# A feed-forward stage in wide units: the first weight sum made by an accumulating DMA instead of a VectorE addition

## The chip, the cores and the metric

One Trainium2 chip, one of its cores. The metric is the device time of one execution in microseconds (us); the median of several runs counts.

## The reference, cut to what matters

One layer of a hybrid backbone over 640 tokens (512 latent, 128 context) with 1024 channels: modulation from a conditioning vector, three mixing branches (neighbourhood attention, mLSTM, short convolution) merged by gates, an output projection, and then the feed-forward stage that the change is in:

```
h2 = rmsnorm(x, P['g_pre_ffn'][l]) * (1 + scale2) + shift2
ff = (jax.nn.silu(h2 @ P['w_ffn_gate'][l]) * (h2 @ P['w_ffn_up'][l])) @ P['w_ffn_down'][l]
x = x + gate2 * rmsnorm(ff, P['g_post_ffn'][l])
```

The gate and up matrices are 1024 x 2816, in float32.

## The kernel before

Every float32 matrix product is made as three products of a high and a low part: ScalarE (ACT) rounds an operand to its high part, VectorE (DVE) subtracts that from the operand for the low part, and TensorE (PE) multiplies high by high, high by low and low by high (lines 2515 to 2517).

The first 256 columns of gate and up are done plainly (units `fg`, `fu`). The rest is done in 20 wide units (`WU`), even ones gate and odd ones up, by a scheme of seven products instead of eight: a unit's weights are two blocks of 128 x 1024, so four quarters a11, a12, a21, a22 of 128 x 512 each. Three sums in the tile `ssum` and one difference in place are made of them (`weight_sums`): s1 = a21 + a22, s2 = s1 - a11, s4 = a12 - s2, and a21 becomes a11 - a21. Each of the seven products q = 0 to 6 takes one operand: 0, 1 and 6 a quarter, 2 takes s2, 3 takes s1, 4 the difference and 5 takes s4. `operand_hi` (ACT, line 1502) and `operand_lo` (DVE, line 2018) split an operand; `snapshot` (ACT, line 1511) copies a partial result out of PSUM; `collect` (DVE, lines 2044, 2057, 2059, 2064) adds results and multiplies gate by up.

A list of steps, PLAN, gives each engine its order. In step `("wu", w, q)` PE makes product q of unit w, while ACT and DVE split the operands of unit w+1 and collect unit w. All engines run their own queue in order and meet at semaphores: `flo_done` counts low parts, `fs_done` the sums, `fp_done` the products, `fsnap` the snapshots. PE's product q = 5 of unit w waits for the third snapshot of the unit (`fsnap`), which stands on ACT's queue behind the high part of s2 of unit w+1.

SyncE's (SP) queue loads the blocks: `load_wide` brings the two blocks of unit w+2 when unit w's last operand is split (line 1096). In units 1 to 8 DVE also makes a piece of the modulation (`ada5_block`, line 2083, two products of 128 x 1024 at the end of step q = 2) from a block that SP loads (line 1099). GpSimd's (POOL) queue has nothing to do in the wide units. `weight_sums` of unit w+1 stands in step q = 0 of unit w, behind the last low part of unit w; for unit 1 it stands in step q = 1 of unit 0.

Of the kernel before, what the change touches and what calls it, by code (L numbers as in the profile page):

```python
# [750 lines left out]
def program(nc, a, out, vline, gline, xline):  # L751

    ctx = ExitStack()
    with ctx:
# [126 lines left out]

        v_out, v_in = sems("v_out v_in")

        ms_one, nat_zero, ml_sc = sems("ms_one nat_zero ml_sc")
        condr0_in, condr0_rd, dot_done, dot_bias, dot_mod = sems(
            "condr0_in condr0_rd dot_done dot_bias dot_mod")
        condr_in, cond_out, ada_done, gcol_rd, gl_tr, gl_row, gl_out, g1_in, g2_in = sems(
# [6 lines left out]

        act_order, dve_order, pool_order = sems("act_order dve_order pool_order")

        cond_zero, cond_rd = sems("cond_zero cond_rd")

        x_sq, x_rstd, x_nrm, x_tr = sems("x_sq x_rstd x_nrm x_tr")
        xt_dve, xt_act = sems("xt_dve xt_act")  # L900

        mod_in, h_aff, h_hid, h_lod = sems("mod_in h_aff h_hid h_lod")
        bias_rd, bias_zero, mv_ones = sems("bias_rd bias_zero mv_ones")


        na_sc, na_max, na_exp, na_prob, na_tr, na_pt, na_pv, na_out = sems(
# [169 lines left out]
        def _(sp):  # L1076
# [44 lines left out]
            for step in PLAN:  # L1121
# [96 lines left out]
        def _(pool):  # L1218
# [11 lines left out]
                return nc.gpsimd.tensor_tensor(dst, dst, neghalf[:, 0:width], ALU.pow)  # L1230

            link(nc.gpsimd.memset(neghalf[:, :], -0.5))
            nc.gpsimd.memset(cond[:, :, :], 0.0).then_inc(cond_zero, 1)
            pool.dma_start(gbias[:, :], a["gbias"]).then_inc(gb_in, 16)
            for t in range(TT):
                pool.wait_ge(x_sq, t + 1)
# [24 lines left out]
            for step in PLAN:  # L1261
# [4 lines left out]
                elif step[0] == "bias0":  # L1266
                    pool.wait_ge(h_lod, KD)
                    pool.wait_ge(gemm_done, gid("mifs", 0, 0, 1) + 1)
                    pool.wait_ge(gemm_done, gid("ada_row", ("first", DOT_CHUNKS[0] - 1)) + 1)
                    nc.gpsimd.memset(bm[:, :, :, 256:NKEY], 0.0).then_inc(bias_zero, 1)  # L1270
                    pool.dma_start(vtok[:, 9, :], a["cache_v"]).then_inc(vc_in, 16)
                    pool.wait_ge(v_out, 16 * CH)
                    for j in range(NQB):
# [11 lines left out]
                elif step[0] == "na" and step[1] == 1 and step[2] in (1, 5, 10):  # L1285
                    hp = {1: 1, 5: 2, 10: 3}[step[2]]
                    bias(hp)
                    if hp < 3:
                        pool.wait_ge(bias_rd, 3 * (hp + 1))
                        load_bias(pool, br_in, hp + 1)  # L1290
                elif step[0] == "mstat":

                    link(nc.gpsimd.tensor_scalar(small[:, 36:40], cols[:, R_MG:R_MG + MH], 0.5, None, ALU.mult))
                    pool.wait_ge(ada_done, EARLY_ADAS)
                    nc.gpsimd.memset(mv[:, :, :, 128:129], 1.0).then_inc(mv_ones, 1)
                    pool.wait_ge(dve_drain, drains("V", gid("kout", 0)))
                    nc.gpsimd.memset(small[0:RW, 42:43], 0.0)
                    nc.gpsimd.memset(st[6][:, :], 1.0).then_inc(ms_one, 1)
                    pool.wait_ge(stored, 32)
                    nc.gpsimd.memset(mnat[:, :].bitcast(F32), 0.0).then_inc(nat_zero, 1)  # L1300
                    pool.wait_ge(na_out, len(NA_UNITS))
                    pool.dma_start(cl[:, :, :], a["state"]).then_inc(state_in, 16)
                elif step[0] == "dots_in":
                    pool.wait_ge(condr0_rd, 1)
                    pool.dma_start(gline[1:2], condr0[0:1, :, :]).then_inc(cond_out, 16)
                elif step[0] == "condr":

                    pool.wait_ge(bo_lod, 12)
                    src = bass.AP(gline.tensor, 2 * D, [[0, P], [D, 2], [1, D]])
                    pool.dma_start(condr[:, :, :], src).then_inc(condr_in, 16)  # L1310
                elif step[0] == "group" and GROUPS[step[1]]["kind"] == "mo":
                    x = GROUPS[step[1]]
                    f, h = x["what"]
                    pool.wait_ge(act_drain, drains("A", step[1]))
                    hd = 2 * UNITS[x["unit"]][1] + f
                    v, w = mo[:, hd, half(h)], small[:, 36 + hd:37 + hd]
                    nc.gpsimd.tensor_scalar(v, v, w, w, ALU.mult, ALU.add).then_inc(mo_rd, 1)
                elif step[0] == "hm" and step[1] == 0:
                    c = step[2]
                    pool.wait_ge(hm_sq, c + 1)  # L1320
                    v = small[:, 16 + 4 * c:20 + 4 * c] if c < 4 else small[:, 32:36]
                    rstd(v, v, 4, 128).then_inc(hm_rstd, 1)
                elif step[0] == "resid":
                    t = step[1]
                    pool.wait_ge(y0_sq, t + 1)
                    v = small[:, 44 + t:45 + t]
                    link(nc.gpsimd.tensor_scalar(v, v, 1.0 / D, EPS, ALU.mult, ALU.add))
                    pool.wait_ge(y_sq, t + 1)
                    link(nc.gpsimd.tensor_scalar(v, small[:, 49 + t:50 + t], 1.0 / D, v, ALU.mult, ALU.add))
                    nc.gpsimd.tensor_tensor(small[:, t:t + 1], v, neghalf[:, 0:1], ALU.pow).then_inc(y_rstd, 1)  # L1330
                elif step[0] == "square2":
                    t = step[1]
# [14 lines left out]
        def _(act):  # L1347
# [143 lines left out]

            def operand_hi(w, q):

                if QUARTER[q] is None:
                    act.wait_ge(fs_done, G_QUADS + 4 * w + {2: 2, 3: 1, 4: 4, 5: 3}[q])
                else:
                    act.wait_ge(fraw_in[w % 2], 32 * (w // 2 + 1))
                if w == 0:
                    wait_release(act, W0 + q // 2)
                else:  # L1500
                    act.wait_ge(fp_done, G_PRODUCTS + 7 * (w - 1) + q + 1)
                nc.scalar.activation(operand(q)[:, 0:512], summand(w, q), ACT.Copy).then_inc(fhi_done, 1)
# [85 lines left out]
                    silu(w, 2)  # L1588

            act.wait_ge(cols_in, 16)  # L1590
            act.wait_ge(cond_zero, 1)
            nc.scalar.activation(cond[:, :, 0:2], cols[:, R_C:R_C + 16].rearrange("p (c k) -> p k c", c=2),
                                 ACT.Silu).then_inc(cond_rd, 1)
            for step in PLAN:
# [209 lines left out]
        def _(dve):  # L1804
# [216 lines left out]
            def weight_sums(w):  # L2021
# [3 lines left out]
                    dve.wait_ge(flo_done, G_OPERANDS + 7 * (w - 1) + 6)  # L2025
                a11, a12, a21, a22 = [quarter(w, j) for j in range(4)]
                s1, s2, s4 = [ssum[:, j, :] for j in range(3)]
                nc.vector.tensor_tensor(s1, a21, a22, ALU.add).then_inc(fs_done, 1)
                dve.wait_ge(fs_done, G_QUADS + 4 * w + 1)
                nc.vector.tensor_tensor(s2, s1, a11, ALU.subtract).then_inc(fs_done, 1)  # L2030
                dve.wait_ge(fs_done, G_QUADS + 4 * w + 2)
                nc.vector.tensor_tensor(s4, a12, s2, ALU.subtract).then_inc(fs_done, 1)
                nc.vector.tensor_tensor(a21, a11, a21, ALU.subtract).then_inc(fs_done, 1)

# [52 lines left out]
            def wide_unit(w, q):  # L2087

                more = w + 1 < WU
                if q == 0:  # L2090
                    if w % 2 == 0 and w:
                        collect(w - 1, 3)
                    operand_lo(w, 6)
                    if more and w:
                        weight_sums(w + 1)
                elif q == 1:
                    if more and w:
                        operand_lo(w + 1, 0)
# [24 lines left out]
            for step in PLAN:  # L2123
# [93 lines left out]
                elif step[0] == "na":  # L2217
                    _, sub, s = step
                    if sub == 0:
# [13 lines left out]
                        if s < len(NA_UNITS):  # L2233
# [6 lines left out]
                                dve.wait_ge(v_out, 16 * CH)  # L2240
                            if kind == "lat":
                                if s == 0:
                                    dve.wait_ge(bias_zero, 1)
                                dve.wait_ge(bias_rd, 3 * hp + BTYPE[j] + 1)
                                for i in range(2):
                                    ins = nc.vector.tensor_tensor_reduce(
# [47 lines left out]
                elif step[0] == "mstat":  # L2294
# [15 lines left out]
                    link(turned(st[0], ib))  # L2310
                    link(turned(st[1], lf))
                    ones = st[6]
                    dve.wait_ge(ms_one, 1)
                    for c in range(TT):
                        ins = nc.vector.tensor_tensor_scan(st[2][:, tok(c)], ones[:, tok(c)], st[1][:, tok(c)], 0.0,
                                                           ALU.mult, ALU.add)
# [187 lines left out]
        def _(pe):  # L2504
# [221 lines left out]
            for step in PLAN:  # L2726
# [100 lines left out]
                elif step[0] == "ml":  # L2827
# [168 lines left out]
```

## Time and profile before

| | |
|---|---|
| median of 3 runs | 1133.09 us (1132.36 to 1133.37) |
| the profiled execution, its own time | 1130.49 us |
| its span in the trace | 1128.6 us |
| PE busy | 1109.5 us (98%) |
| DVE busy | 770.4 us (68%) |
| ACT busy | 522.5 us (46%) |
| POOL busy | 94.6 us (8%) |
| mean traffic of the DMA engines | 116 GB/s |
| granted TensorE clock over the span | 1.00 |

The busy share is an average over stages. The wide units stand from 725 us to about 972 us of the span. The chain that ended last is PE's for 92% of the span, so an instruction of another engine matters only where PE waits for it.

### The profile page before, as it was taken

The numbers are of one execution on the slowest core, as the hardware profiler recorded it, in microseconds if no ns is written. First come the engines' busy times: TensorE is split into PE (matmuls) and PEld (weight loads), VectorE is DVE, ScalarE is ACT, GpSimd is POOL, SyncE is SP. The second block draws the span as 40 slices with busy tenths as digits, with TensorE's granted clock in tenths as the row PEclk, the third lists the DMA queues.
The fourth block names the chain that finished last, engine by engine and source line by source line (L and its number), as shares of the span: only waits on it lengthen the run. The fifth ranks groups of instructions, "written<-read, shape, count | busy, mean of one in ns | idle before, by whom it ended". The sixth has DMA issues, their size and how long they took to land.

```text
span 1128.6 us, 18734 instructions
## 1 busy us (share of the span) xinstructions
PE 1109.5 (98%) x7228; PEld 1043.2 (92%) x7228; DVE 770.4 (68%) x1415; ACT 522.5 (46%) x1024; POOL 94.6 (8%) x126
## 2 busy tenths in 40 slices
PE   6999999999999999999999999999999999999997
PEld 4799999889999999999999988999999999988886
DVE  5726778449675666977778856899997777633444
ACT  5534444344334333655453438555555555533431
POOL 2051211000000000810000002000000000000002
PEclk9999999999999999999999999999999999999999
DMA  9694444232431121122233665043422232315112
GB/s 370 242 242 172 133 140 142 75 94 76 80 72 57 57 69 63 39 94 76 81 125 101 209 204 172 9 168 131 143 83 75 83 143 75 123 66 184 56 38 94
DMA packets 40327, 131.28 MB, mean 116 GB/s; under 512 B 8768, under 2 KB 10352, under 8 KB 38576
## 3 DMA queue, kind: packets, MB, share of 16 engines
q1 hardware_dynamic: 36592, 121.41, 33.0%
q0 software_dynamic: 3648, 8.68, 2.6%
q8 instruction: 58, 0.95, 0.3%
q14 instruction: 29, 0.24, 0.1%
HBM read 122.69 MB, written 7.37 MB: 115 GB/s over the span
## 4 chain that ended last, share of the span: by engine, by line
PE 92%; DVE 4%; ACT 1%; issue 1%; DMA 0%; POOL 0%; SPq 0%; POOLq 0%; ACTq 0%; DVEq 0%
PE ps L2515 28%; PE ps L2516 28%; PE ps L2517 28%; PE ps L2773 1%; PE ps L2812 1%; PE ps L2796 1%; PE ps L2860 1%; PE ps L2862 1%; PE ps L2864 1%; DMA xt<-in_x_sample 0%; PE ps L2586 0%; PE ps L2740 0%; PE ps L2847 0%; DVE h_lo L2485 0%; PE ps L2845 0%
## 5 line engine op out<-in xcount | busy, mean ns | idle before, releaser
L2517 PE MATMUL ps<-h_hi,w_lo 128*128 128x320 f32 x992 | 306.5, 309 | 0.0
L2515 PE MATMUL ps<-h_hi,w_hi 128*128 128x320 f32 x832 | 263.1, 316 | 0.2 <-DVE w_hi L2018 0.2
L2516 PE MATMUL ps<-h_lo,w_hi 128*128 128x320 f32 x832 | 257.0, 309 | 0.0
L2517 PEld LDWEIGHTS ps<-h_hi,w_lo 128*128 128x128 f32 x992 | 186.2, 188 | 0.0
L2515 PEld LDWEIGHTS ps<-h_hi,w_hi 128*128 128x128 f32 x832 | 156.3, 188 | 2.4 <-DVE w_hi L2018 0.5
L2516 PEld LDWEIGHTS ps<-h_lo,w_hi 128*128 128x128 f32 x832 | 156.4, 188 | 0.1
L2515 PE MATMUL ps<-w_hi,h_hi 128*128 128x512 f32 x378 | 149.3, 395 | 0.0
L2517 PE MATMUL ps<-w_hi,h_lo 128*128 128x512 f32 x378 | 147.3, 390 | 0.0
L2516 PE MATMUL ps<-w_lo,h_hi 128*128 128x512 f32 x378 | 147.1, 389 | 0.0
L1817 DVE TENSOR_TENSOR w_lo<-raw,w_hi 128x1024 fp32r<-128x1024 f32 x85 | 102.9, 1222 | 52.7 <-ACT w_hi L1368 51.9
L1368 ACT ACTIVATE w_hi<-raw 128x1024 fp32r<-128x1024 f32 x85 | 88.3, 1050 | 20.4 <-PE ps L2517 20.3
L2515 PE MATMUL ps<-h_hi,w_lo 128*128 128x320 f32 x304 | 94.2, 310 | 0.8 <-ACT snap L1511 0.8
L2516 PE MATMUL ps<-h_lo,w_lo 128*128 128x320 f32 x304 | 93.9, 309 | 0.0
L2515 PEld LDWEIGHTS ps<-w_hi,h_hi 128*128 128x128 f32 x378 | 71.0, 188 | 16.4 <-issue 1.6
L2517 PEld LDWEIGHTS ps<-w_hi,h_lo 128*128 128x128 f32 x378 | 71.0, 188 | 15.1
L2516 PEld LDWEIGHTS ps<-w_lo,h_hi 128*128 128x128 f32 x378 | 71.0, 188 | 14.0
L1877 DVE TENSOR_TENSOR h_lo<-ff,h_hi 128x1280 fp32r<-128x1280 f32 (+1 forms) x22 | 30.5, 1428 | 64.4 <-ACT h_hi L1396 64.4
L2515 PE MATMUL ps<-tt_hi,w_hi 128*128 128x320 f32 x240 | 74.2, 309 | 0.0
L2516 PE MATMUL ps<-tt_lo,w_hi 128*128 128x320 f32 x240 | 74.2, 309 | 0.0
L2517 PE MATMUL ps<-tt_hi,w_hi 128*128 128x320 f32 x240 | 74.2, 309 | 0.0
L1511 ACT ACTIVATE snap<-ps 128x320 f32<-128x320 f32 x80 | 34.9, 437 | 63.6 <-PE ps L2517 63.6
L1396 ACT ACTIVATE h_hi<-ff 128x1280 fp32r<-128x1280 f32 (+1 forms) x22 | 25.7, 1217 | 71.8 <-PE ps L2517 71.8
(340 smaller groups left out, 2233.5 us busy)
## 6 DMA issues: line engine op xcount, KB each, us to landing
raw<-in_w_blocks SPq DMA_DIRECT2D x182, 512.0 KB, 3.7
ada<-in_w_first SPq DMA_DIRECT2D x8, 1024.0 KB, 19.6
xline<-x SPq DMA_DIRECT2D x5, 512.0 KB, 5.1
x<-xline SPq DMA_DIRECT2D x5, 512.0 KB, 7.9
xt<-in_x_sample SPq DMA_DIRECT2D x4, 512.0 KB, 5.7
vtok<-vline POOLq DMA_DIRECT2D x8, 256.0 KB, 9.0
g<-gline SPq DMA_DIRECT2D x2, 1024.0 KB, 7.6
xb<-in_x_sample SPq DMA_DIRECT2D x4, 512.0 KB, 4.8
```

The source lines that it names most:

```text
L1368: ins = nc.scalar.activation(held(w_hi, b), raw[:, s, :], ACT.Copy)
L1396: nc.scalar.activation(h_hi[:, o2 + k:o2 + k + n, :], ff[:, k0 + k:k0 + k + n, :], ACT.Copy).then_inc(ffs_hi, 1)
L1511: nc.scalar.activation(snap[:, i, :], wbank(w, 1 if i == 2 else 0), ACT.Copy).then_inc(fsnap, 1)
L1817: nc.vector.tensor_tensor(held(w_lo, b), raw[:, s, :], held(w_hi, b).bitcast(F32), ALU.subtract).then_inc(lo_done, 1)
L1877: nc.vector.tensor_tensor(h_lo[:, o2 + k:o2 + k + n, :], ff[:, k0 + k:k0 + k + n, :], h_hi[:, o2 + k:o2 + k + n, :].bitcast(F32), ALU.subt ...
L2515: nc.tensor.matmul(dst, wh, xh, start=first, stop=False, skip_group_check=resumed)
L2516: nc.tensor.matmul(dst, wh, xl, start=False, stop=False, skip_group_check=resumed)
L2517: return nc.tensor.matmul(dst, wl, xh, start=False, stop=last, skip_group_check=resumed)
L2773: ins = nc.tensor.matmul(dst[:, NKEY:512], src, pt[:, n % 2, i, c * P:(c + 1) * P], start=(c == 0), stop=(c == 2))
L2796: nc.tensor.matmul(A[i][:, 0:256], q, kk, start=True, stop=True)
L2812: ins = nc.tensor.transpose(A[2 + i][:, c * P:(c + 1) * P], sx[:, n % 2, i, c * P:(c + 1) * P], ident)
L2860: ins = nc.tensor.matmul(A[3][:, pr], st_sb[:, b, i, :], mv[:, ch, hd, :], start=True, stop=True)
```

## The change

For each of the 20 wide units, s1 is no longer a DVE addition. SP first loads the quarter a21 of the unit from the weights in device memory into the first third of `ssum` (`load_first_sum`), once the previous unit's operand 3, which reads the old s1, has its low part. Then POOL's queue starts a DMA that reads a22 from device memory and adds it to what lies there. DVE's s2 and ACT's high part of operand 3 wait for that DMA (`s1_sum`); the count of `fs_done` in a unit falls from four to three. From unit 2 on the rest of `weight_sums` moves on DVE's queue from step q = 0 to step q = 2, behind the low parts of operands 0 and 1 and ahead of `ada5_block`; for unit 1 it stays in step q = 1 of unit 0. Five semaphores that POOL's early fills raised become one counter, `pool_fills`.

```diff
@@ SP
+            def load_first_sum(w):
+                if w:
+                    sp.wait_ge(flo_done, G_OPERANDS + 7 * (w - 1) + 4)
+                else:
+                    sp.wait_ge(n2_tr, 2 * TT)
+                src = a["w_blocks"][STORED_AT[WU_PLACES[2 * w + 1]]]
+                sp.dma_start(ssum[:, 0, :], src[:, 0:512]).then_inc(s1_in, 16)
...
+                elif step[0] == "tsum":
+                    load_first_sum(0)
+                elif step[0] == "wop" and step[2] == 5:
+                    load_first_sum(1)
+                elif step[0] == "wu" and step[2] == 5 and step[1] + 2 < WU:
+                    load_first_sum(step[1] + 2)
@@ POOL
+                elif step[0] == "tsum" or step[0] == "wu" and step[2] == 0 and step[1] + 1 < WU:
+                    w = step[1] + 1 if step[0] == "wu" else 0
+                    src = a["w_blocks"][STORED_AT[WU_PLACES[2 * w + 1]]]
+                    pool.wait_ge(s1_in, 16 * (w + 1))
+                    pool.dma_start(ssum[:, 0, :], src[:, 512:1024], accum_op=ALU.add).then_inc(s1_sum, 16)
@@ ACT, operand_hi
-                if QUARTER[q] is None:
-                    act.wait_ge(fs_done, G_QUADS + 4 * w + {2: 2, 3: 1, 4: 4, 5: 3}[q])
+                if q == 3:
+                    act.wait_ge(s1_sum, 16 * (w + 1))
+                elif QUARTER[q] is None:
+                    act.wait_ge(fs_done, G_QUADS + 3 * w + {2: 1, 4: 3, 5: 2}[q])
@@ DVE, weight_sums
-                nc.vector.tensor_tensor(s1, a21, a22, ALU.add).then_inc(fs_done, 1)
-                dve.wait_ge(fs_done, G_QUADS + 4 * w + 1)
+                dve.wait_ge(s1_sum, 16 * (w + 1))
                 nc.vector.tensor_tensor(s2, s1, a11, ALU.subtract).then_inc(fs_done, 1)
@@ DVE, wide_unit
                     operand_lo(w, 6)
-                    if more and w:
-                        weight_sums(w + 1)
...
                     if more:
                         operand_lo(w + 1, 1)
+                        if w:
+                            weight_sums(w + 1)
                     if 1 <= w <= KD:
                         ada5_block(w - 1)
```

DVE's queue in unit 1, before, from the low part of operand 6 of unit 1 (`w_hi<-raw`) to the low parts of operands 2 and 3 of unit 2:

```order
L2018 TENSOR_TENSOR w_hi<-raw,w_hi 128x512 [waits fhi_done]
L2028 TENSOR_TENSOR ssum<-raw 128x512 [waits flo_done,fraw_in0]
L2030 TENSOR_TENSOR ssum<-ssum,raw 128x512 [waits fs_done]
L2032 TENSOR_TENSOR ssum<-raw,ssum 128x512 [waits fs_done]
L2033 TENSOR_TENSOR raw<-raw 128x512
L2018 TENSOR_TENSOR w_hi<-raw,w_hi 128x512 [waits fhi_done]
L2059 TENSOR_TENSOR snap<-ps,snap 128x320 [waits fp_done,fsnap]
L2064 TENSOR_TENSOR ff<-snap,sg 128x320 [waits t_lod,fsg,fz]
L2018 TENSOR_TENSOR w_lo<-raw,w_lo 128x512 [waits fhi_done]
L2083 SCALAR_TENSOR_TENSOR prod_152,gcol<-raw_151,condr 128x1024 [waits condr_in,raw5_in0]
L2083 SCALAR_TENSOR_TENSOR prod_153,gcol<-raw_151,condr 128x1024
L2018 TENSOR_TENSOR w_hi<-ssum,w_hi 128x512 [waits fhi_done]
```

The same place with the change (the first row stands for the low parts of operand 6 of unit 1 and operand 0 of unit 2, now next to each other):

```order
L2041 TENSOR_TENSOR w_hi<-raw,w_hi 128x512 [waits fhi_done] x2
L2081 TENSOR_TENSOR snap<-ps,snap 128x320 [waits fp_done,fsnap]
L2086 TENSOR_TENSOR ff<-snap,sg 128x320 [waits t_lod,fsg,fz]
L2041 TENSOR_TENSOR w_lo<-raw,w_lo 128x512 [waits fhi_done]
L2052 TENSOR_TENSOR ssum<-ssum,raw 128x512 [waits s1_sum,flo_done,fraw_in0]
L2054 TENSOR_TENSOR ssum<-raw,ssum 128x512 [waits fs_done]
L2055 TENSOR_TENSOR raw<-raw 128x512
L2105 SCALAR_TENSOR_TENSOR prod_152,gcol<-raw_151,condr 128x1024 [waits condr_in,raw5_in0]
L2105 SCALAR_TENSOR_TENSOR prod_153,gcol<-raw_151,condr 128x1024
L2041 TENSOR_TENSOR w_hi<-ssum,w_hi 128x512 [waits fhi_done]
```

The addition is gone, the three that are left have moved behind two low parts and a collect, and the first of them now waits for a DMA.

SP's queue with the change, from the last blocks of units 0 and 1 through the beginning of the wide units (`raw_151` is the modulation's block; lines 1097 and 1109 are 1096 and 1099 of before):

```order
L1097 DMA raw<-in_w_blocks 128x1024 [waits lo_done] x2
L1106 DMA ssum<-in_w_blocks 128x512 [waits n2_tr]
L1106 DMA ssum<-in_w_blocks 128x512 [waits flo_done]
L1097 DMA raw<-in_w_blocks 128x1024 [waits flo_done]
L1097 DMA raw<-in_w_blocks 128x1024
L1109 DMA raw_151<-in_w_blocks 128x1024 x2
L1106 DMA ssum<-in_w_blocks 128x512 [waits flo_done]
L1097 DMA raw<-in_w_blocks 128x1024 [waits flo_done]
```

The rows of line 1106 are new; the others stand in their old order.

## Rows read from the trace of the kernel before

**Rows 1.** The page: busy shares and the chain that ended last.
```profile
PE 1109.5 (98%) x7228; PEld 1043.2 (92%) x7228; DVE 770.4 (68%) x1415; ACT 522.5 (46%) x1024; POOL 94.6 (8%) x126
...
PE 92%; DVE 4%; ACT 1%; issue 1%; DMA 0%; POOL 0%; SPq 0%; POOLq 0%; ACTq 0%; DVEq 0%
```

**Rows 2.** Busy us by stretch: about units 0, 1 and 9.
```profile
core 0: us, PE busy (x) PEld busy (x) DVE busy (x) ACT busy (x) POOL busy (x), PEclk, DMA share, GB/s
725.20:739.05 13.85, 13.07 (x86) 12.66 (x87) 13.78 (x22) 7.58 (x15) 0.00 (x0) 1.00 0.41 151
739.05:751.34 12.29, 12.29 (x86) 12.29 (x85) 10.98 (x20) 7.00 (x15) 0.00 (x0) 1.00 0.37 123
...
837.41:849.71 12.30, 12.30 (x86) 12.30 (x86) 9.70 (x19) 6.17 (x13) 0.00 (x0) 1.00 0.26 87
```

**Rows 3.** The waits of PE: total us, times, longest us.
```profile
PE ps L2515 <- ACT snap L1511: 0.8, 1, 0.8
...
PE ps L2515 <- DVE w_hi L2018: 0.2, 1, 0.2
```

**Rows 4.** Timeline of DVE in unit 0: start us, us, what.
```profile
728.08 0.68 DVE L2018 TENSOR_TENSOR w_lo<-ssum,w_lo 128x512 fp32r<-128x512 f32 x1
...
732.68 0.68 DVE L2028 TENSOR_TENSOR ssum<-raw 128x512 f32<-128x512 f32 x1
733.40 0.69 DVE L2030 TENSOR_TENSOR ssum<-ssum,raw 128x512 f32<-128x512 f32 x1
...
735.34 0.68 DVE L2018 TENSOR_TENSOR w_hi<-raw,w_hi 128x512 fp32r<-128x512 f32 x1
```

**Rows 5.** Timeline of ACT in unit 0.
```profile
734.12 0.63 ACT L1502 ACTIVATE w_hi<-ssum 128x512 fp32r<-128x512 f32 x1 [0.85 <-DVE ssum L2030]
734.66 0.42 ACT L1511 ACTIVATE snap<-ps 128x320 f32<-128x320 f32 x1
```

**Rows 6.** Timeline of PE: product 5 and product 6 of unit 0.
```profile
735.23 0.38 PE L2515 MATMUL ps<-h_hi,w_lo 128*128 128x320 f32 x1 [0.77 <-ACT snap L1511]
...
737.05 0.31 PE L2515 MATMUL ps<-tt_hi,w_hi 128*128 128x320 f32 x1
```

**Rows 7.** Landings: page and window at 66.9 us: issue, count, KB, median us to landing.
```profile
raw<-in_w_blocks SPq DMA_DIRECT2D x182, 512.0 KB, 3.7
...
vtok<-vline POOLq DMA_DIRECT2D x1, 256.0 KB, 2.6
...
vtok<-in_cache_v POOLq DMA_DIRECT2D x1, 256.0 KB, 7.8
...
cols<-in_cols SPq DMA_DIRECT2D x1, 68.0 KB, 1.9
```

**Rows 8.** The page: DMA queues: packets, MB, share of 16 engines.
```profile
q0 software_dynamic: 3648, 8.68, 2.6%
```

**Rows 9.** Timeline of DVE in unit 1.
```profile
741.70 0.68 DVE L2028 TENSOR_TENSOR ssum<-raw 128x512 f32<-128x512 f32 x1
...
744.36 0.68 DVE L2018 TENSOR_TENSOR w_hi<-raw,w_hi 128x512 fp32r<-128x512 f32 x1
744.96 0.48 DVE L2059 TENSOR_TENSOR snap<-ps,snap 128x320 f32<-128x320 f32 x1
...
746.48 1.22 DVE L2083 SCALAR_TENSOR_TENSOR prod<-raw,condr 128x1024 f32<-128x1024 f32 x1
...
749.38 0.68 DVE L2018 TENSOR_TENSOR w_lo<-ssum,w_lo 128x512 fp32r<-128x512 f32 x1
```

**Rows 10.** Timeline of ACT in unit 1.
```profile
742.59 0.63 ACT L1502 ACTIVATE w_lo<-raw 128x512 fp32r<-128x512 f32 x1 [0.69 <-PE ps L2517]
...
746.05 0.44 ACT L1511 ACTIVATE snap<-ps 128x320 f32<-128x320 f32 x1 [0.80 <-PE ps L2517]
```

**Rows 11.** A POOL transfer beside a busy DVE: its landing, and the engines.
```profile
condr<-gline POOLq DMA_DIRECT2D x1, 1024.0 KB, 4.7
...
570.00:576.00 6.00, 6.00 (x43) 6.00 (x42) 4.28 (x10) 2.02 (x4) 0.62 (x1) 1.00 0.65 250
```

More of the change, by code:

```diff
@@ L882, in program @@
         v_out, v_in = sems("v_out v_in")
-        ms_one, nat_zero, ml_sc = sems("ms_one nat_zero ml_sc")
+        ml_sc, pool_fills = sems("ml_sc pool_fills")
         condr0_in, condr0_rd, dot_done, dot_bias, dot_mod = sems(
@@ L895, in program @@
         act_order, dve_order, pool_order = sems("act_order dve_order pool_order")
-        cond_zero, cond_rd = sems("cond_zero cond_rd")
+        cond_rd = sem("cond_rd")
         x_sq, x_rstd, x_nrm, x_tr = sems("x_sq x_rstd x_nrm x_tr")
@@ L902, in program @@
         mod_in, h_aff, h_hid, h_lod = sems("mod_in h_aff h_hid h_lod")
-        bias_rd, bias_zero, mv_ones = sems("bias_rd bias_zero mv_ones")
+        bias_rd = sem("bias_rd")
         na_sc, na_max, na_exp, na_prob, na_tr, na_pt, na_pv, na_out = sems(
@@ L931, in program @@
         raw5_in = sems("raw5_in0 raw5_in1")
+        s1_in, s1_sum = sems("s1_in s1_sum")
         ts_done, t_hid, t_lod = sems("ts_done t_hid t_lod")
@@ L1232, in _ @@
             link(nc.gpsimd.memset(neghalf[:, :], -0.5))
-            nc.gpsimd.memset(cond[:, :, :], 0.0).then_inc(cond_zero, 1)
+            nc.gpsimd.memset(cond[:, :, :], 0.0).then_inc(pool_fills, 1)
             pool.dma_start(gbias[:, :], a["gbias"]).then_inc(gb_in, 16)
@@ L1269, in _ @@
                     pool.wait_ge(gemm_done, gid("ada_row", ("first", DOT_CHUNKS[0] - 1)) + 1)
-                    nc.gpsimd.memset(bm[:, :, :, 256:NKEY], 0.0).then_inc(bias_zero, 1)
+                    nc.gpsimd.memset(bm[:, :, :, 256:NKEY], 0.0).then_inc(pool_fills, 1)
                     pool.dma_start(vtok[:, 9, :], a["cache_v"]).then_inc(vc_in, 16)
@@ L1294, in _ @@
                     pool.wait_ge(ada_done, EARLY_ADAS)
-                    nc.gpsimd.memset(mv[:, :, :, 128:129], 1.0).then_inc(mv_ones, 1)
+                    nc.gpsimd.memset(mv[:, :, :, 128:129], 1.0).then_inc(pool_fills, 1)
                     pool.wait_ge(dve_drain, drains("V", gid("kout", 0)))
                     nc.gpsimd.memset(small[0:RW, 42:43], 0.0)
-                    nc.gpsimd.memset(st[6][:, :], 1.0).then_inc(ms_one, 1)
+                    nc.gpsimd.memset(st[6][:, :], 1.0).then_inc(pool_fills, 1)
                     pool.wait_ge(stored, 32)
-                    nc.gpsimd.memset(mnat[:, :].bitcast(F32), 0.0).then_inc(nat_zero, 1)
+                    nc.gpsimd.memset(mnat[:, :].bitcast(F32), 0.0).then_inc(pool_fills, 1)
                     pool.wait_ge(na_out, len(NA_UNITS))
@@ L1590, in _ @@
             act.wait_ge(cols_in, 16)
-            act.wait_ge(cond_zero, 1)
+            act.wait_ge(pool_fills, 1)
             nc.scalar.activation(cond[:, :, 0:2], cols[:, R_C:R_C + 16].rearrange("p (c k) -> p k c", c=2),
@@ L2027, in weight_sums @@
                 s1, s2, s4 = [ssum[:, j, :] for j in range(3)]
-                nc.vector.tensor_tensor(s1, a21, a22, ALU.add).then_inc(fs_done, 1)
-                dve.wait_ge(fs_done, G_QUADS + 4 * w + 1)
+                dve.wait_ge(s1_sum, 16 * (w + 1))
                 nc.vector.tensor_tensor(s2, s1, a11, ALU.subtract).then_inc(fs_done, 1)
-                dve.wait_ge(fs_done, G_QUADS + 4 * w + 2)
+                dve.wait_ge(fs_done, G_QUADS + 3 * w + 1)
                 nc.vector.tensor_tensor(s4, a12, s2, ALU.subtract).then_inc(fs_done, 1)
@@ L2242, in _ @@
                                 if s == 0:
-                                    dve.wait_ge(bias_zero, 1)
+                                    dve.wait_ge(pool_fills, 2)
                                 dve.wait_ge(bias_rd, 3 * hp + BTYPE[j] + 1)
@@ L2312, in _ @@
                     ones = st[6]
-                    dve.wait_ge(ms_one, 1)
+                    dve.wait_ge(pool_fills, 4)
                     for c in range(TT):
@@ L2343, in _ @@
                     dve.wait_ge(stored, 32)
-                    dve.wait_ge(nat_zero, 1)
+                    dve.wait_ge(pool_fills, 5)
                     link(turned(ib, st[0]))
@@ L2852, in _ @@
                         if n == 0:
-                            pe.wait_ge(mv_ones, 1)
+                            pe.wait_ge(pool_fills, 3)
                             pe.wait_ge(gl_row, 1)
```

## The prediction

> **What bounds the kernel now.** I read the page first: PE is busy for 98% of the span and is 92% of the chain that ended last, DVE is 4% of it [rows 1]. Then the busy times by unit: a wide unit's stretch of 12.3 us is full on PE, while DVE has 10.98 in unit 1 and 9.70 in unit 9, and only about unit 0 are both short of time, PE 13.07 of 13.85 and DVE 13.78 [rows 2]. PE's waits say what that gap is: in all the wide units PE waits 0.8 us for ACT's snapshot and 0.2 us for DVE's first operand, once each [rows 3]. So the most that a lighter DVE can give back here is 1.0 us, 0.09% of the time. The question is what the new chain of two DMAs does to engines that are on time today.
>
> The rhythm is needed for that. Product 6 of unit 0 starts at 737.05 [rows 6], and ACT's third snapshot of unit 1, which waits for the end of product 3, starts at 746.05 [rows 10]; five products lie between, so a product is near 1.76 and a unit 12.3. Unit 1 starts at 738.8, its product 5 at 738.8 + 5 x 1.76 = 747.6.
>
> **What is removed.** Twenty additions, of 0.68 each with 0.72 from one start to the dependent next one (732.68 to 733.40) [rows 4]: 20 x 0.7 = 14 us of DVE. They are hidden behind PE but for unit 0. Moving the three others behind two low parts brings those forward, and PE does not wait for these either (above), so that is worth nothing. Merging five semaphores changes no order and no wait: nothing.
>
> **What is added.** Per unit one load on SP of 256 KB (L us from issue to landing) and then one accumulating DMA of POOL, 256 KB (A us). The second cannot start before the first has landed, and the first not before the low part of the previous operand 3. POOL has nothing else in this stage and SP is parked at the same waits as before. Issue follows a semaphore closely; I allow 0.05 a hop.
>
> L: 68 KB land in 1.9 and 512 KB in 3.7 [rows 7]; a line between them gives 2.7 for 256 KB, and these two are its bounds. A: no accumulate stands in this trace. Below it cannot be under a plain 256 KB transfer of this queue, 2.6 when that queue was free; from above the nearest is the other 256 KB load of the queue, 7.8, in a crowd [rows 7]. This queue's packets took 2.6% of 16 engines' span, 0.026 x 16 x 1128.6 = 470 us for 3648 packets, 0.129 each [rows 8]. 256 KB in rows of 2 KB is 128 packets, 8 for each DMA engine, 1.0 us. The accumulate has to read the destination as well, so I add these packets once more: A = 3.6, nearer the row of 2.6, since the DMA engines are free most of the time here (share 0.37 in unit 1 [rows 2]). The Trainium skill (Collectives: The Full Stack, the bandwidth ceiling) says the same of the mechanism: an add in the DMA engine costs not for its arithmetic but for its second source read, which halves the rate. By that rule the data part doubles, and the sum is the one given below; without it the plain 2.6 would stand and the sum would be 1.0 lower. No row here shows an accumulate.
>
> **Unit 0 (the sums of unit 1).** The low part of operand 3 of unit 0 ends at 728.08 + 0.68 = 728.76 [rows 4]; with the first sum gone ahead of it on a DVE without a pause, at 728.1. SP issues the load of unit 1's a21. s1 is complete at 728.1 + 0.05 + 2.7 + 0.05 + 3.6 = 734.5, and s2 starts at 734.55 in place of 733.40 [rows 4]: 1.15 late. Behind it: s2 to ACT's high part 0.72 (733.40 to 734.12), that to the snapshot 0.54 (to 734.66), 0.42 for it [rows 5], and PE's product 5 follows at 735.23 [rows 6]. This chain has no slack today (it is the 0.8 us wait of [rows 3]), so the 1.15 goes to PE in full, and what the earlier first operand gives (0.2) is lost in the same wait. With A = 2.6 the price is 0.15, and with A = 7.8 it is 5.35. Nothing queued behind DVE's wait is late next: operand 0 of unit 1 has its low part at 734.55 + 1.94 + 0.68 = 737.2, before unit 1.
>
> **Units 1 to 8.** With the change DVE in unit 1 starts the collect when product 1 has ended (742.6, where ACT's high part starts [rows 10]). A collect is 0.92: it starts at 744.96, and the modulation at 746.48 has one low part of 0.60 ahead (744.36 to 744.96) [rows 9]. So the low part of operand 1 starts at 743.5 and s2 could start at 744.1. From s2's start it is 1.94 for the three sums (733.40 to 735.34 [rows 4]), 2.90 for the modulation and operand 2 (746.48 to 749.38) and 0.68 for operand 3 [rows 9], together 5.5: the low part of operand 3 ends at 749.6. Then the next load is issued, and the next s2 could start at 744.1 + 12.3 = 756.4. So L + A has 756.4 - 749.6 - 0.1 = 6.7 us, against 2.7 + 3.6 = 6.3. It fits with 0.4 to spare: price nothing. The cover ends at A = 4.0. Past it each unit is late by the excess against the one before. PE has further slack: s1 to the end of the third snapshot is 0.05 + 0.72 + 0.54 + 0.44 [rows 4, 5, 10] = 1.75, which must be before 747.6, so s1 at 745.85, where s2 could start at 744.1: 1.75 of lateness is free once, then every unit pays its excess in full.
>
> **Units 9 to 19.** There the modulation (2.3) is gone from the loop: L + A has 12.3 - 3.2 - 0.1 = 9.0. Price nothing for A up to 6.3.
>
> **The sum.** 1.15 - 0 = +1.15 us on the profiled execution: 1130.49 + 1.15 = 1131.6. That execution lies 2.6 under the median of 1133.09; on the median the sum is **1134.2 us**. A measurement of this kernel tells about 0.2%, 2.3 us, from no change.
>
> **The rivals.**
> First, the loop of units 1 to 8 is too tight and the change is slower. It decides from L + A = 6.7 and lives where DVE waits for s1 and ACT's snapshot stands behind s2. Eight times the excess, less the 1.75, plus unit 0's delay. A = 4.6: 8 x 0.6 - 1.75 = 3.05, and 2.15 for unit 0: +5.2, 1138.3. A = 5.6: 8 x 1.6 - 1.75 = 11.05, and 3.15: +14.2, 1147.3. For it speaks that the margin is only 0.4 of a sum with an unseen A, that SP's modulation load of 512 KB (3.7 [rows 7]) is issued some 1 us before it, and that the wide loads of 1 MB overlap the accumulate's tail; against it the light traffic of 123 GB/s in unit 1 [rows 2].
>
> Second, POOL's transfer is held up while DVE works, so that A is as in a crowd, 7.8 [rows 7]. Then all units pay: 8 x 3.8 - 1.75 = 28.65, unit 0 5.35, ten more units at 1.5 each: +49, 1182. Against it: a POOL transfer of 1024 KB landed in 4.7 beside a DVE that was busy for 4.28 of 6 us [rows 11]. The Trainium skill (SBUF — State Buffer, two separate sides) has this as a trap: the descriptors of POOL's DMAs cannot be written while a DVE operation holds the shared port. It names copies in a two-port mode; the wide units have almost none. By that rule in its narrow form nothing happens, in a wide form this rival does. I give it one chance in ten.
>
> Third, the change does what it says and DVE's relief reaches PE: if L + A were under 5.2, s1 of unit 1 would be there by 733.4 and the two waits of [rows 3] would begin to close, at best 1.0 us faster, 1132.1. That is still no change that can be told. To be faster by 0.2% PE would have to gain 2.3 us, which its waits in this stage don't hold.
>
> **How the numbers follow.** Forecast, hidden but for unit 0 (with the third): 0.51. Tight loop: 0.36. Held up: 0.10. Something else, faster by over 0.2%: 0.03. The forecast's own range is 1132.1 to 1135.4. For eight in ten it starts at 1132.3 and takes in most of the tight loop, up to 1149 (A near 5.7), leaving out the held-up case. Faster 0.03, same 0.50, slower 0.47: part of the tight loop with A barely over 4 stays inside 0.2%.
>
> **What would show it.** POOL's 20 DMAs land in 3 to 4 us; DVE waits for a DMA once, about 2 us, in unit 0; PE's wait for the snapshot in unit 0 is near 2 us in place of 0.77; units 1 to 19 take 12.3 us each. Wrong would be: landings over 4 us, DVE idle before s2 in units 1 to 8, PE waits for L1534's snapshot in each, and units of over 12.3 us.

## The result, and the profile after

The changed kernel takes 1156.6 us (median of 6 runs, 1155.5 to 1158.05) against 1132.34 of the kernel before on the same chips (6 runs, 1130.99 to 1133.37): ratio 1.0217, interval 1.0206 to 1.0228. It is slower by 24 us, where 1 was forecast, and the time lies outside the range. The profiled execution took 1157.39, its span 1155.5, 26.9 more than before.

The page, rows as in [rows 1, 7, 8]:

```profile
PE 1118.2 (97%) x7228; PEld 1050.2 (91%) x7228; DVE 760.9 (66%) x1395; ACT 521.3 (45%) x1024; POOL 112.5 (10%) x146
...
q0 software_dynamic: 6528, 13.92, 5.5%
...
PE 82%; DMA 7%; DVE 6%; issue 2%; ACT 1%; POOL 0%; SPq 0%; POOLq 0%; DVEq 0%; ACTq 0%
...
ssum<-in_w_blocks SPq DMA_DIRECT2D x20, 256.0 KB, 2.9
ssum<-in_w_blocks POOLq DMA_DIRECT2D x20, 256.0 KB, 4.3
```

DVE is lighter by 9.5 us, and yet the chain that ended last gives DVE 6% and DMA 7%, where DMA had 0%. The median of 4.3 for the accumulate misleads: it is over all 20, and half of them are in units where nothing waits for them.

The waits of PE, DVE and ACT (engine and line, what it waited for, total us, times, longest):

```profile
ACT w_hi L1525 <- DVE ssum L2052: 32.7, 9, 5.3
...
DVE ssum L2052 <- DMA ssum<-in_w_blocks: 30.8, 10, 5.0
...
PE ps L2537 <- ACT snap L1534: 18.4, 9, 5.1
```

PE's one wait of 0.8 for the snapshot [rows 3] has become nine of 18.4 in all, and the 0.2 for the first operand is gone. Read upwards from PE's row, it goes back by steps: PE waits for ACT's snapshot, ACT for s2, DVE before s2 (L2052) for the accumulate. PE's account of the 26.9 us: 18.4 - 0.8 - 0.2 = 17.4 of waits and 1118.2 - 1109.5 = 8.7 of busy time with the same 7228 matmuls, 26.1 together.

Where in time it lies, from the products of the wide units alone (matmuls with `tt_hi`; count, ns least, median and most, first and last start). First before, then after:

```profile
L2517 PE MATMUL ps<-tt_hi,w_hi x240: 309/309/309, 729.1 to 972.9; 128*128 128x320 f32 x120
```

```profile
L2539 PE MATMUL ps<-tt_hi,w_hi x240: 303/309/472, 729.5 to 999.8; 128*128 128x320 f32 x120
```

243.8 us became 270.3: all but 0.4 of the loss is between these rows. The longest matmul is 472 ns where it was 309.

DVE's timeline has s2 (one a unit; the bracket is its idle time before it):

```profile
737.87 0.69 DVE L2052 TENSOR_TENSOR ssum<-ssum,raw 128x512 f32<-128x512 f32 x1 [5.04 <-DMA ssum<-in_w_blocks]
750.99 0.69 DVE L2052 TENSOR_TENSOR ssum<-ssum,raw 128x512 f32<-128x512 f32 x1
767.22 0.69 DVE L2052 TENSOR_TENSOR ssum<-ssum,raw 128x512 f32<-128x512 f32 x1 [4.11 <-DMA ssum<-in_w_blocks]
782.04 0.70 DVE L2052 TENSOR_TENSOR ssum<-ssum,raw 128x512 f32<-128x512 f32 x1 [2.54 <-DMA ssum<-in_w_blocks]
797.17 0.69 DVE L2052 TENSOR_TENSOR ssum<-ssum,raw 128x512 f32<-128x512 f32 x1 [3.95 <-DMA ssum<-in_w_blocks]
...
871.18 0.69 DVE L2052 TENSOR_TENSOR ssum<-ssum,raw 128x512 f32<-128x512 f32 x1 [2.31 <-DMA ssum<-in_w_blocks]
...
894.35 0.68 DVE L2052 TENSOR_TENSOR ssum<-ssum,raw 128x512 f32<-128x512 f32 x1
```

From the second row to 871.18 are eight units: 120.2 us, 15.0 each where 12.3 was the unit's time, 21.8 too many. The first row is unit 0's: s2 was forecast at 734.55 and comes at 737.87. At the end, with the modulation gone from the loop, nothing waits.

The load, the accumulate, s2 and what DVE does up to the next low part of operand 3 form a ring: each waits for the one before it, and the low part frees the buffer for the next load. One turn of the ring, unit 4, from the timelines of SP, POOL and DVE, one after the other:

```profile
786.38 0.33 SPq L1109 DMA_DIRECT2D raw<-in_w_blocks  x1
787.59 0.33 SPq L1106 DMA_DIRECT2D ssum<-in_w_blocks  x1
791.65 0.80 SPq L1097 DMA_DIRECT2D raw<-in_w_blocks  x2
...
791.22 0.87 POOL L1343 DMA_DIRECT2D ssum<-in_w_blocks  x1 [14.04 <-DMA ssum<-in_w_blocks]
...
786.87 0.69 DVE L2041 TENSOR_TENSOR w_lo<-ssum,w_lo 128x512 fp32r<-128x512 f32 x1
...
802.00 0.68 DVE L2041 TENSOR_TENSOR w_lo<-ssum,w_lo 128x512 fp32r<-128x512 f32 x1
```

and how long the two transfers took to land, by the issues of the windows 787.5 to 787.7 and 791.20 to 791.27, then an accumulate of a late unit, issued at 888.75:

```profile
ssum<-in_w_blocks SPq DMA_DIRECT2D x1, 256.0 KB, 3.4
...
ssum<-in_w_blocks POOLq DMA_DIRECT2D x1, 256.0 KB, 5.8
...
ssum<-in_w_blocks POOLq DMA_DIRECT2D x1, 256.0 KB, 4.0
```

So the turn reads: the low part of operand 3 ends at 787.56; 0.03 to SP's issue; 3.4 for the load; 0.23 to POOL's issue; 5.8 for the accumulate (797.02); 0.15 to s2 (797.17); 5.5 to the end of the next low part of operand 3 (802.68). Sum 15.1, the unit's time. The last 5.5 is what the prediction had. The transfers are 3.4 + 5.8 = 9.2 with hops of 0.4, where 6.7 was the room that the prediction had. And 0.4 us behind the accumulate SP issues the next 1 MB of wide blocks (791.65), which runs beside all of it. The late unit's accumulate lands in 4.0.

### The profile page after: what moved, and what is told of

It is laid out like the page before. It is cut to its first block, busy times and chain, and to the rows that moved or that the text cites. A ratio compares the mean times of both kernels' runs of the same rounds, so it can differ in the third digit from the quotient of the medians.

```text
span 1155.5 us, 18755 instructions
## 1 busy us (share of the span) xinstructions
PE 1118.2 (97%) x7228; PEld 1050.2 (91%) x7228; DVE 760.9 (66%) x1395; ACT 521.3 (45%) x1024; POOL 112.5 (10%) x146
## 4 chain that ended last, share of the span: by engine, by line
PE 82%; DMA 7%; DVE 6%; issue 2%; ACT 1%; POOL 0%; SPq 0%; POOLq 0%; DVEq 0%; ACTq 0%
PE ps L2537 25%; PE ps L2538 24%; PE ps L2539 24%; DMA ssum<-in_w_blocks 6%; PE ps L2795 1%; PE ps L2834 1%; PE ps L2818 1%; PE ps L2882 1%; PE ps L2884 1%; DVE ssum L2052 1%; PE ps L2886 1%; DVE w_lo L2041 1%; DMA xt<-in_x_sample 1%; PE ps L2608 0%; PE ps L2762 0%
## 5 line engine op out<-in xcount | busy, mean ns | idle before, releaser
L2539 PE MATMUL ps<-h_hi,w_lo 128*128 128x320 f32 x992 | 308.6, 311 | 0.0
L2539 PEld LDWEIGHTS ps<-h_hi,w_lo 128*128 128x128 f32 x992 | 188.0, 190 | 0.0
L2537 PE MATMUL ps<-h_hi,w_lo 128*128 128x320 f32 x304 | 96.9, 319 | 18.4 <-ACT snap L1534 18.4
L1389 ACT ACTIVATE w_hi<-raw 128x1024 fp32r<-128x1024 f32 x85 | 88.3, 1050 | 20.4 <-PE ps L2539 20.3
L2537 PEld LDWEIGHTS ps<-h_hi,w_lo 128*128 128x128 f32 x304 | 58.6, 193 | 20.5 <-issue 20.5
L2041 DVE TENSOR_TENSOR w_hi<-raw,w_hi 128x512 fp32r<-128x512 f32 x60 | 41.1, 688 | 29.5 <-ACT w_hi L1525 29.5
```

Of the source, the lines that this page charges most:

```text
L1389: ins = nc.scalar.activation(held(w_hi, b), raw[:, s, :], ACT.Copy)
L2041: nc.vector.tensor_tensor(v[:, 512:1024], summand(w, q), v[:, 0:512].bitcast(F32), ALU.subtract).then_inc(flo_done, 1)
L2537: nc.tensor.matmul(dst, wh, xh, start=first, stop=False, skip_group_check=resumed)
L2539: return nc.tensor.matmul(dst, wl, xh, start=False, stop=last, skip_group_check=resumed)
```

## The experiments

Eight kernels, in two groups. The kernel before took 1131.74 (21 runs) beside the first four and 1131.81 (7 runs) beside the others. The forecasts of the second four take the turn of the ring as 15.3 us; it is 15.0.

**two_buffers.** The odd units' s1 gets a tile of its own, so both transfers are a unit ahead and out of the ring.

```
+        s1b = at("s1b", [P, 512], R1 + 55296)
+        def s1_of(w):
+            return s1b[:, :] if w % 2 else ssum[:, 0, :]
...
-                if w:
-                    sp.wait_ge(flo_done, G_OPERANDS + 7 * (w - 1) + 4)
+                if w > 1:
+                    sp.wait_ge(flo_done, G_OPERANDS + 7 * (w - 2) + 4)
...
-                elif step[0] == "wu" and step[2] == 5 and step[1] + 2 < WU:
-                    load_first_sum(step[1] + 2)
                 elif step[0] == "wu" and step[2] == 0:
+                    if w + 2 < WU:
+                        load_first_sum(w + 2)
```

> s1 gets a second tile, so that a unit's load and accumulate no longer wait for the low part of the previous operand 3; both are started a unit earlier; every DMA of the change stays. Theory one (the loop: one buffer ties low part of operand 3, load, accumulate and s2 into a ring that is longer than 12.3 us): DVE never waits for s1, PE's waits for the snapshot vanish, the clock stays full, 1131 to 1133 us. Theory two (the traffic itself: 40 more transfers and POOL's descriptors slow PE, DVE or the wide loads): the loss mostly stays, over 1145 us.

It takes 1129.9 (1128.75 to 1132.13, 11 runs), ratio 0.998, interval 0.9971 to 0.9989. Its windows about units 0 and 1 (us, then PE, PEld, DVE, ACT, POOL busy, granted clock, DMA share, GB/s), and DVE's timeline:

```profile
725.00:740.00 15.00, 15.00 (x103) 14.79 (x102) 14.93 (x24) 9.45 (x17) 0.87 (x1) 1.00 0.34 99
740.00:755.00 15.00, 15.00 (x105) 15.00 (x104) 13.54 (x26) 8.21 (x17) 0.87 (x1) 1.00 0.72 235
```

```profile
735.03 0.68 DVE L2059 TENSOR_TENSOR ssum<-s1b,raw 128x512 f32<-128x512 f32 x1
...
745.77 0.69 DVE L2059 TENSOR_TENSOR ssum<-ssum,raw 128x512 f32<-128x512 f32 x1
...
757.81 0.68 DVE L2059 TENSOR_TENSOR ssum<-s1b,raw 128x512 f32<-128x512 f32 x1
```

No bracket stands before s2, PE is full in both windows, and its two waits of [rows 3] are gone: the loss was the ring's, since the transfers still take as long (4.2 to 6.8 for the accumulates of units 1 to 8). So the first theory holds, though the time is 1.1 us under its range. It is the only version that is clearly ahead of both kernels. Of its 1.8 us, the closed waits explain 1.0; its trace can't show the rest, since the profiled execution (1132.13) is the slowest of the eleven.

**plain_second.** POOL copies a22 instead of adding it; s1 is then a22 alone, and that addition is left out of the computation. Same bytes written, one source.

```
-                    pool.dma_start(ssum[:, 0, :], src[:, 512:1024], accum_op=ALU.add).then_inc(s1_sum, 16)
+                    pool.dma_start(ssum[:, 0, :], src[:, 512:1024]).then_inc(s1_sum, 16)
```

> POOL's DMA copies a22 over a21 in place of adding it (s1 is then a22 alone, the rest is as it is). Theory one: only A falls, from 4.0 to about 2.8 when the engines are free and from 5.8 to about 4.5 beside the wide loads; the ring loses 1.3 us or more per unit, 1136 to 1148 us. Theory two (traffic): the same bytes come from device memory, only the read of the destination is gone, so near 1156 us.

1141.28 (4 runs), ratio 1.0086 [1.0067, 1.0105]. POOL's issue in its timeline, the landing of that issue, and DVE's wait:

```profile
883.82 0.54 POOL L1343 DMA_DIRECT2D ssum<-in_w_blocks  x1 [11.87 <-DMA ssum<-in_w_blocks]
```

```profile
ssum<-in_w_blocks POOLq DMA_DIRECT2D x1, 256.0 KB, 2.9
```

```profile
DVE ssum L2052 <- DMA ssum<-in_w_blocks: 13.9, 8, 3.1
```

The issue takes 0.54 instead of 0.87, the transfer 2.8 to 3.4 free and 3.5 to 3.8 beside the wide loads (5.0 once, at 759.41). The time lies in the range of the first theory, but beside the wide loads the copy saves 2 us, not the 1.3 that was assumed. Even with this transfer the kernel loses 9.5 us (3.0 of them in unit 0's wait), and from 777.30 to 829.03 a turn still takes 12.9; so the ring of two transfers does not fit, added or not, and adding makes up the other 15 us.

**ada_late.** DVE's modulation pieces move from just behind the sums to behind the low part of operand 3, which takes 2.3 us out of the ring.

```
                             weight_sums(w + 1)
-                    if 1 <= w <= KD:
-                        ada5_block(w - 1)
                 elif q in (3, 4):
                         operand_lo(w + 1, q - 1)
+                    if q == 4 and 1 <= w <= KD:
+                        ada5_block(w - 1)
```

SP's load of the sum also goes ahead of the modulation's load (the edit of **swap** below).

> DVE's modulation piece stands behind the low part of operand 3 in place of ahead of operand 2, and SP's load of a21 stands ahead of the load of the modulation's block. Theory one: the ring of units 1 to 8 loses 2.3 us and the crowd ahead of its load, so it fits into 12.3 us or misses it by little; what stays is unit 0's stall of 4 to 5 us and the low clock right behind it: 1137 to 1143 us. Theory two (traffic): over 1150 us.

1138.82 (4 runs), ratio 1.0053 [1.0037, 1.007]. Waits, and the windows of units 0, 1 and 2:

```profile
PE ps L2537 <- ACT snap L1534: 5.0, 1, 5.0
...
DVE ssum L2052 <- DMA ssum<-in_w_blocks: 5.0, 1, 5.0
```

```profile
725.00:740.00 15.00, 10.98 (x75) 10.67 (x73) 9.93 (x16) 6.25 (x13) 0.89 (x1) 0.99 0.41 115
740.00:755.00 15.00, 13.97 (x78) 14.00 (x79) 11.23 (x19) 7.86 (x17) 0.87 (x1) 0.78 0.53 166
755.00:770.00 15.00, 15.00 (x104) 15.00 (x103) 13.74 (x25) 7.37 (x15) 0.87 (x1) 1.00 0.55 148
```

One wait is left, unit 0's. All the others are gone, and with them 17 us of the loss. SP's order alone is worth 1 us (swap), so the place of DVE's piece decides; but the fit is close. In units 2 and 3 the accumulates land at 764.07 and 776.58, and s2 starts 0.4 and 0.5 later without a wait. The load took 2.8 and 2.9 there, where it takes 3.4 in unit 4 of the changed kernel, so whether the move fits without SP's edit is not shown. Unit 0's wait alone costs 7.1 of median: 4.0 of waits (5.0 in place of 0.8 and 0.2), and most of the remainder is PE's matmuls at a granted clock of 0.78 in the window behind the wait, 78 matmuls in 13.97 us where 104 pass in 15.00 (PE is busy for 1113.4 us in all, 3.9 more than before).

**move_alone.** The kernel before, with only the place of the four additions moved.

```
-                    if more and w:
-                        weight_sums(w + 1)
...
+                        if w:
+                            weight_sums(w + 1)
```

> The kernel before with its three and one additions moved from step 0 to step 2 of a unit, s1 still by DVE, no DMA added. Both theories: within 0.2% of before; a loss here would mean that the move and not the DMA costs.

1131.64 (10 runs), ratio 0.9997 [0.9988, 1.0006]: the move is free, as the prediction had it.

**first_only.** Only unit 1's sum has a second tile and is made early; all later ones as in the change (diff as in two_buffers, with `w == 1` for `w % 2` and the load of unit 1 behind that of unit 0). It asks whether unit 0's pause starts the lateness of the rest.

> Only unit 1's sum gets the second tile and is made early; all others keep the one buffer and the ring. If unit 0's wait and the low clock right behind it are worth the 7 us that the run with the late modulation had left, this run gives those back and nothing else: 1148 to 1151 us. Rival: the low clock after unit 0's wait is what also starts the lateness of units 2 to 8 (without it the ring would fit): then under 1142 us.

1152.09 (4 runs), ratio 1.0179 [1.0164, 1.0194]. Window and waits:

```profile
725.00:740.00 15.00, 15.00 (x103) 14.78 (x102) 13.80 (x22) 10.06 (x21) 0.00 (x0) 1.00 0.44 149
```

```profile
DVE ssum L2059 <- DMA ssum<-in_w_blocks: 27.9, 10, 4.8
...
PE ps L2544 <- ACT snap L1541: 14.1, 8, 3.7
```

Unit 0 is clean, at full clock, and 20.3 us remain, 1.1 above the range; so unit 0's pause adds 4.0 to the changed kernel, not the 7.1 of ada_late. The difference is the low clock behind it, which costs next to nothing when the ring, and not PE, sets the pace right after (a reading, not tested by itself). The rival is refuted: the ring runs late by itself, from unit 1 on.

**wide_wait.** SP issues the wide blocks only when the accumulate of the next unit has landed.

```
                     sp.wait_ge(flo_done, G_OPERANDS + 7 * w + 7)
+                    if w + 1 < WU:
+                        sp.wait_ge(s1_sum, 16 * (w + 2))
```

> SP issues the wide loads only when the accumulate has landed, so nothing runs beside it. If the crowd is what makes the accumulate 5.8 us in place of 4.1, the period falls from 15.3 to 13.5 and unit 0's wait by 1.5 us: 1138 to 1143. Rival: the accumulate is slow for another reason (DVE's work holds up POOL's descriptors, or the low clock): its landings stay at 5.5 to 6 us and the time near 1156.

1143.09 (1141.46 to 1144.98, 4 runs), ratio 1.0098 [1.0078, 1.0118]. The time lies at the upper end of its forecast, 0.1 past it. A landing (issue at 786.59), and s2 in DVE's timeline:

```profile
ssum<-in_w_blocks POOLq DMA_DIRECT2D x1, 256.0 KB, 4.3
```

```profile
777.43 0.69 DVE L2054 TENSOR_TENSOR ssum<-ssum,raw 128x512 f32<-128x512 f32 x1 [1.39 <-DMA ssum<-in_w_blocks]
...
790.97 0.69 DVE L2054 TENSOR_TENSOR ssum<-ssum,raw 128x512 f32<-128x512 f32 x1 [2.36 <-DMA ssum<-in_w_blocks]
```

Alone, the accumulates land in 4.0 to 4.3 instead of 5.4 to 6.7, and a unit takes 13.3 instead of 15.0 (the same eight turns). The loss goes from 24.3 to 11.3: 13.0 us are given back by the order of SP's transfers alone, so what the overlap with the wide loads adds was about half of it. What is left is the ring that does not fit even so (13.2 to 13.6 in units 2 to 7, 0.9 to 1.3 too long), and unit 0, whose wait is 3.6. The accumulate issued at 759.99 landed in 4.1; first the 0.86 us of POOL's issue, then the time to its landing:

```profile
759.99:760.85 0.86, 0.86 (x8) 0.86 (x7) 0.86 (x3) 0.63 (x1) 0.86 (x1) 1.00 0.00 0
759.99:764.10 4.11, 4.11 (x30) 4.11 (x29) 1.82 (x4) 1.43 (x3) 0.86 (x1) 1.00 0.45 64
```

DVE is busy throughout POOL's issue, and the transfer is as quick as any. In the changed kernel DVE was busy for 2.83 of the 4.1 us of the accumulate at 901.23 and for only 2.00 of the 5.8 of the one at 791.22. So DVE's work does not hold POOL's transfer up.

**swap.** Only SP's order: the load of the sum ahead of the modulation's load. **swap_wait.** That and the wait of wide_wait.

```
-                elif step[0] == "wu" and step[2] == 5 and step[1] + 2 < WU:
-                    load_first_sum(step[1] + 2)
...
-                    elif w < KD - 1:
+                    if w + 2 < WU:
+                        load_first_sum(w + 2)
+                    if 0 < w < KD - 1:
                         sp.wait_ge(ada5_done, w)
```

> SP's load of a21 stands ahead of the load of the modulation's block instead of 1.2 us behind it. The ring's period was 15.3 us, with 3.4 for this load. If the crowd ahead of it costs 0.5 us, the period falls to 14.8 and the time by 3 to 4 us: 1152 to 1154. Rival: the modulation's block is then late itself and DVE waits for it: no gain, 1156 or more.

> Both edits. Period 5.5 + 2.9 + 0.3 + 4.1 = 12.8 us, 0.5 over a unit: 1134 to 1139 us, of which 3 to 4 are unit 0's. Rival: the two crowds are one, so that the second edit adds nothing to the better of the two.

1155.35 (1150.26 to 1158.28, 4 runs; ratio 1.0201 [1.0171, 1.0232]) and 1141.97 (1141.03 to 1143.2, 4 runs; 1.0089 [1.0073, 1.0104]). Both missed, though the second's rival came near. The four runs of swap spread over 8 us, so its gain of 1 us is not clear of noise. The load still took 3.1 to 3.5 in units 2 to 6 of it (2.7 in unit 7; in unit 2 it fell from 4.9 to 3.1), though the modulation's block of 512 KB was now issued behind it. But only 0.4 us behind: the two still run side by side. Where that block comes 2.3 us later (ada_late, units 2 to 7) the load takes 2.7 to 2.9, once 3.4, and where there is none (the changed kernel, units 8 to 13) 2.7 to 3.0, against 3.2 to 3.5 with it 1.2 us ahead (units 3 to 7). That points to the block as what makes 3.4 out of 2.9; no run tests it alone. On top of wide_wait the swap is worth 1 us or nothing.

## Why the prediction was wrong

**What bounds the kernel, and DVE's relief.** Right in the main. PE bounds it: two_buffers keeps the relief without the ring, both waits of [rows 3] are closed, and it gains 1.8 where 1.0 was the most that the prediction allowed; 0.8 of it is unexplained.

**What is removed and moved.** Right: move_alone is unchanged.

**Unit 0.** The mechanism was right, with no slack and PE held up in full; the size was off. "s1 is complete at 728.1 + 0.05 + 2.7 + 0.05 + 3.6 = 734.5": the load was issued 0.7 later, at 728.84 (the DVE work ahead of it began 0.8 later in this execution, 719.69 against 718.92, which used up the relief), and took 2.9, the hop to POOL 0.3, the accumulate 5.7 in place of 3.6, beside SP's four blocks of 512 KB (the issues of 725 to 740; the blocks too land later, in 6.6 where the same four took 5.1 before; first before, then after):

```profile
raw<-in_w_blocks SPq DMA_DIRECT2D x4, 512.0 KB, 5.1
```

```profile
raw<-in_w_blocks SPq DMA_DIRECT2D x4, 512.0 KB, 6.6
ssum<-in_w_blocks SPq DMA_DIRECT2D x1, 256.0 KB, 2.9
ssum<-in_w_blocks POOLq DMA_DIRECT2D x1, 256.0 KB, 5.7
```

The term of 1.15 measured 4.1 in PE's wait (5.06 for 0.77, less the 0.2). With the low clock behind it, for which the prediction had no term, it is 7.1 where nothing hides that (ada_late) and 4.0 in the changed kernel (first_only).

**Units 1 to 8.** Here the step failed: "So L + A has 756.4 - 749.6 - 0.1 = 6.7 us, against 2.7 + 3.6 = 6.3. It fits with 0.4 to spare: price nothing." The room was right: the 5.5 behind s2 came out to the tenth, and 12.3 less 5.5 is 6.8. The other side was not. L was 3.4, the hops 0.4 and A 5.8, 9.6 in all where 6.8 are free, and 15.0 instead of 12.3 a unit. The signs of being wrong that the prediction named (landings over 4 us, idle time before s2, waits for L1534's snapshot, units of over 12.3 us) came with it from unit 2 on. Three errors stand in that sum. L was a line between two transfers of other sizes, not a transfer in this ring. A counted packets at the mean rate of a queue but sized a transfer as if alone, while the prediction itself named "the wide loads of 1 MB" as overlapping its tail, and put them among the rival's arguments in place of the price. And a margin of 0.4 on two estimated transfers was priced at nothing in the sum, though a loss there is paid in every unit.

**A feedback that no part had.** SP issues the wide loads after the low part of operand 6 of the unit, at a time that follows PE and not the sum. When the sum is late it slides under them, and they make it later. In unit 1 the accumulate is issued at 745.18, 2.4 us ahead of the wide loads, and lands in 4.1; in unit 8 it is 0.9 ahead and lands in 4.3; in units 3 to 7 it is 0.2 to 0.6 ahead and lands in 5.6 to 6.7. wide_wait cuts the loop and gets 13 us of 24 back. ada_late has its accumulates 3 us ahead of the wide loads in units 2 and 3 (759.17 against 762.42, 771.58 against 774.64) and gets 17 back; they land in 4.9 and 5.0 and not in 4.1, and there the modulation's block was issued 0.8 and 0.9 us ahead of them.

**The rivals.** The first was what happened, in its place: DVE waits for s1, ACT's snapshot stands behind s2. Its formula with the excess as measured, 15.0 - 12.3 = 2.7, is 8 x 2.7 - 1.75 = 19.9, with 4.1 for unit 0 24.0: the measured medians differ by 24.3. first_only, without unit 0's pause, lost 20.3 against the 19.9. The range ended at an A near 5.7, and A did measure 5.8; what carried the time past 1149 is the 0.7 more for the load and the 0.3 more for the hops, paid eight times.

The second, POOL held up while DVE works, is refuted by wide_wait. Of the Trainium skill's trap (SBUF — State Buffer, two separate sides), in the wide form that the prediction gave a chance, no run shows a sign: wide_wait's accumulates land in 4.0 to 4.3, the one at 759.99 in 4.1 with DVE busy for all 0.86 us of POOL's issue.

The third never had its condition. two_buffers, which has both waits closed, gained 1.8 for its 1.0.

The estimate for the second read held where it applied. Free transfers land in 4.0 to 4.3 when they add and 2.8 to 3.4 when they copy, 1.1 apart, against the 1.0 that was added. The Trainium skill (Collectives: The Full Stack, the bandwidth ceiling) gives the second source read as an add's cost, and the trace agrees in size, though it does not isolate the read: POOL's own issue is 0.3 longer for an accumulate (0.87 against 0.54), which may be part of the 1.1. Beside the wide loads the difference is 5.4 to 6.7 against 3.5 to 3.8, twice as much.

**Units 9 to 19.** Right but for unit 9, whose s2 (871.18) still waits 2.31 and has the last modulation in its turn of the ring; from there on DVE waits once more, for 0.19.

**Open.** Whether the modulation's block is what makes the load 3.4; which resource the accumulate and the wide loads contend for; the 0.8 us of two_buffers' gain beyond the closed waits; and what the low clock costs in units 2 to 8, where the ring sets the pace and a slow PE partly hides in it (its 8.7 us of extra busy time are no price of their own).

## What to carry to other kernels

When an operation becomes a transfer in a ring (buffer free, load, transfer, use), price each transfer beside what the other queues issue in the same microseconds, and take a margin smaller than the spread of its landings as a loss in every turn. What cured this ring was a second buffer: 2 KB a partition turned +24 us into -1.8, while a shorter transfer (plain_second) left 9.5. And read the landings of the units that wait, not the page's median over all.

## What the runs showed of the hardware

The granted clock after a pause of PE. Behind unit 0's wait of 5 us PE restarts with matmuls of 0.47 us, 0.27 apart, at a granted clock of 0.50, the 1.2 GHz level; from about 744.9 they take 0.31 and start 0.15 apart, at 2.4 GHz:

```profile
739.69 0.60 PE L2537 MATMUL ps<-h_hi,w_lo 128*128 128x320 f32 x1 [5.06 <-ACT snap L1534]
...
740.36 0.47 PE L2539 MATMUL ps<-h_hi,w_lo 128*128 128x320 f32 x1
740.63 0.47 PE L2537 MATMUL ps<-h_hi,w_lo 128*128 128x320 f32 x1
...
746.83 0.31 PE L2539 MATMUL ps<-h_hi,w_hi 128*128 128x320 f32 x1
746.98 0.31 PE L2537 MATMUL ps<-h_hi,w_hi 128*128 128x320 f32 x1
```

The first 4.8 us of this, and the two windows from 740 and from 800 of the changed kernel, with the clock at 0.84 and 0.90 in the mean:

```profile
740.00:744.80 4.80, 4.80 (x19) 4.80 (x19) 4.24 (x8) 2.26 (x6) 0.00 (x0) 0.50 0.38 137
740.00:755.00 15.00, 15.00 (x88) 15.00 (x88) 11.35 (x19) 7.18 (x17) 0.86 (x1) 0.84 0.44 131
800.00:815.00 15.00, 13.63 (x84) 13.40 (x84) 10.10 (x19) 6.08 (x14) 0.87 (x1) 0.90 0.50 141
```

88 matmuls pass where 104 do at full clock, with PE busy for all 15 us. Shorter waits did it too: behind those of 2.1, 2.6 and 2.4 us that ended at 769.05, 799.00 and 829.41 PE again starts 12 to 14 matmuls 0.27 apart, while behind those of 1.4 us and less, and one of 2.1 (845.60), the clock stays at 1.00. The four slow stretches hold 59 such starts, 0.12 too long each: 7.1 of the 8.7 us by which PE's busy time grew. So a stall of PE can cost more than its length: some 3 us on top of 4 in ada_late.
